# Two attention mixers re-sequenced: score pairs between projections, and latent keys one turn sooner

## The reference, cut to what matters

```python
# differential attention, 8 heads: two score maps per head, one weighted difference
s1 = einsum("bqhd,bkhd->bhqk", q1, k1) * scale
s2 = einsum("bqhd,bkhd->bhqk", q2, k2) * scale
p = softmax(s1) - lam * softmax(s2)
o = einsum("bhqk,bkhe->bqhe", p, v)          # then rms_norm, w_o

# latent attention (MLA), 16 heads, 256 queries, 512 keys
cq, ckv, k_rope = split(h @ w_down, [256, 384])
q = rms_norm(cq) @ w_uq                      # 64 + 32 (rotary) per head
kv = rms_norm(ckv) @ w_ukv                   # 64 key + 64 value columns per head
s = (q_nope @ k_nope + rope(q_rope) @ rope(k_rope)) * scale
o = softmax(s) @ v
```

## Time and profile before

| | us |
|---|---|
| three runs | 2319.05, 2320.97, 2321.87 |
| median | 2320.97 |
| the profiled execution, whole | 2318.96 |
| its span | 2317.1 |
| PE busy | 2124.6 (92%) |
| DVE busy | 1500.3 (65%) |
| ACT busy | 1039.8 (45%) |

### The profile page before, as it was taken

One profiled execution on the slowest core, in us unless ns is written; L12 is line 12 of the kernel. 1 busy time (PEld: TensorE's weight loads), 2 busy tenths in 40 slices (PEclk: granted clock), 3 DMA queues, 4 the chain that ended last, 5 costly groups with the idle time before them and its releaser, 6 DMA issues.

```text
span 2317.1 us, 33662 instructions
## 1 busy us (share of the span) xinstructions
PE 2124.6 (92%) x12966; PEld 1849.5 (80%) x12966; DVE 1500.3 (65%) x2165; ACT 1039.8 (45%) x1740; POOL 7.2 (0%) x30
## 2 busy tenths in 40 slices
PE   5989999998999889999987889997899889999997
PEld 2677888885777768888866679996899787799997
DVE  3358676686666577767777767885766654555554
ACT  4325223235566552322335655554544563444444
POOL 0000000000000000000000000000000000000000
PEclk8999999998999999999988999998999987799998
DMA  9634464442111136458551037671455531355551
GB/s 352 234 116 141 145 206 144 155 136 78 55 55 55 60 141 199 141 189 274 189 134 55 28 119 244 233 238 58 143 185 181 154 109 45 102 173 177 177 179 58
DMA packets 254192, 339.27 MB, mean 146 GB/s; under 512 B 23943, under 2 KB 232162, under 8 KB 254066
## 3 DMA queue, kind: packets, MB, share of 16 engines
q1 hardware_dynamic: 254066, 337.54, 44.2%
HBM read 336.47 MB, written 1.05 MB: 146 GB/s over the span
## 4 chain that ended last, share of the span: by engine, by line
PE 86%; DVE 6%; ACT 5%; issue 2%; DMA 1%; SPq 1%; POOL 0%; DVEq 0%; ACTq 0%
PE bank L1350 26%; PE bank L1351 25%; PE bank L1352 25%; PE bank L1968 4%; DMA mod_raw<-in_mod_w 1%; DVE norm L2048 1%; PE bank L1400 1%; PE bank L1573 1%; PE bank L1412 1%; SPq L530 0%; PE bank L1426 0%; PE bank L1890 0%; PE bank L1891 0%; ACT norm L813 0%; DVE mpt_lo L2506 0%
## 5 line engine op out<-in xcount | busy, mean ns | idle before, releaser
L1350 PE MATMUL bank<-h_hi,w_hi 128*128 128x256 f32 (+3 forms) x2024 | 673.1, 333 | 53.4 <-DVE h_lo L2057 48.6
L781 ACT ACTIVATE w_hi<-w_raw 128x1024 fp32r<-128x1024 f32 x443 | 464.8, 1053 | 525.6 <-PE bank L1352 505.1
L1351 PE MATMUL bank<-h_lo,w_hi 128*128 128x256 f32 (+3 forms) x2024 | 666.4, 329 | 0.0
L1352 PE MATMUL bank<-h_hi,w_lo 128*128 128x256 f32 (+3 forms) x2024 | 665.6, 329 | 0.0
L2024 DVE TENSOR_TENSOR w_lo<-w_raw,w_hi 128x1024 fp32r<-128x1024 f32 x443 | 539.7, 1222 | 172.1 <-ACT w_hi L781 169.6
L1350 PEld LDWEIGHTS bank<-h_hi,w_hi 128*128 128x128 f32 (+1 forms) x2024 | 392.1, 194 | 99.7 <-issue 59.3
L1352 PEld LDWEIGHTS bank<-h_hi,w_lo 128*128 128x128 f32 (+1 forms) x2024 | 391.8, 194 | 32.3
L1351 PEld LDWEIGHTS bank<-h_lo,w_hi 128*128 128x128 f32 (+1 forms) x2024 | 392.4, 194 | 31.0 <-issue 0.2
L1350 PE MATMUL bank<-g_hi,w_hi 128*128 128x512 f32 (+1 forms) x1152 | 391.1, 339 | 4.5 <-DVE g_lo L2341 3.0
L1351 PE MATMUL bank<-g_lo,w_hi 128*128 128x512 f32 (+1 forms) x1152 | 388.4, 337 | 0.0
L1352 PE MATMUL bank<-g_hi,w_lo 128*128 128x512 f32 (+1 forms) x1152 | 388.2, 337 | 0.0
(11 more groups left out here) (356 smaller groups left out, 2363.0 us busy)
## 6 DMA issues: line engine op xcount, KB each, us to landing
w_raw<-in_mlp_w SPq DMA_DIRECT2D x128, 1024.0 KB, 5.7
mod_raw<-in_mod_w SPq DMA_DIRECT2D x128, 768.0 KB, 5.2
w_raw<-in_w_expert_gate SPq DMA_DIRECT2D x16, 1024.0 KB, 5.2
w_raw<-in_w_expert_up SPq DMA_DIRECT2D x16, 1024.0 KB, 5.2
w_raw<-in_w_expert_down SPq DMA_DIRECT2D x16, 1024.0 KB, 4.9
w_raw<-in_diff_w_qkv SPq DMA_DIRECT2D x12, 1024.0 KB, 5.2
w_raw<-in_fourier_w SPq DMA_DIRECT2D x8, 1024.0 KB, 8.3
w_raw<-in_w_in SPq DMA_DIRECT2D x8, 1024.0 KB, 5.8
```

The source lines that it names most:

```text
L781: act.activation(W_hi[n % RING][:, :].rearrange("p (k c) -> p k c", c=P), w_raw[slot][:, :, place, :], ACT.Copy).then_inc(s("w_hi"), 1)
L1350: pe.matmul(dst, w_hi, r_hi, start=start, stop=False)
L1351: pe.matmul(dst, w_hi, r_lo, start=False, stop=False)
L1352: return pe.matmul(dst, w_lo, r_hi, start=False, stop=stop)
```

## The change

Six edits, all in the two mixers.

1. Differential attention, PE: the four score pairs of a head are issued one at a time or two together, as 0, then 1 and 2, then 3, with the panels (and halves of panels, `panel_part`) between them; `turn_weights` now stands in the middle of panel v. `exps` and `mixes` are called for (0,) and (1, 2, 3), and ACT takes the projected q between them.
2. The last head: pairs 0 and 1, `out_products(0)`, pair 2, `out_products(1)`, pair 3, `out_products(2)`; `exps` and `mixes` run over all four in one call.
3. Down projection: the rotary keys are rotated before the reciprocal of the keys' norm, the square sum of the keys is issued in the middle of the third panel, and the queries' reciprocal and table come before the low part of `ckv` and a panel split. ACT's copies move likewise. `query_sum` stands ahead of the first query on PE.
4. The low part of the rotary keys (two 64x512 subtractions) moves from DVE to POOL, between POOL's two rotary swaps of weights.
5. Keys of a pair of heads are projected in the even turn before last instead of the last odd one, and their high and low parts are made half (one head) per turn.
6. `mpt_hi` and `mpt_lo` have two buffers, and on ACT and DVE the copies of the transposed weights come after the output of head t-2.

```diff
-        if turn % 2:
-            add("k", (turn + 1) // 2, "mla_k_lo", turn + 3)
+        if turn % 2 == 0 and turn // 2 + 1 < MLA_HEADS // 2:
+            add("k", turn // 2 + 1, "mla_k_lo", turn + 4)
...
-        mpt_hi, mpt_lo = sb("mpt_hi", [P, 4, LAT], F32R), sb("mpt_lo", [P, 4, LAT], F32R)
+        mpt_hi = [sb("mpt_hi0", [P, 4, LAT], F32R), sb("mpt_hi1", [P, 4, LAT], F32R, over=at["norm0"])]
+        mpt_lo = [sb("mpt_lo0", [P, 4, LAT], F32R), sb("mpt_lo1", [P, 4, LAT], F32R, over=at["norm2"])]
...
             swap_rotary(u, 0)
+            pool.wait_ge(s("kr_hi"), 1)
+            pool.wait_ge(s("uq_swapped"), 1)
+            pool.tensor_tensor(mk_lo[0][HALF:P, :], kr_f[HALF:P, :], mk_hi[0][HALF:P, :].bitcast(F32),
+                               ALU.subtract).then_inc(s("kr_lo"), 1)
...
+            pool.wait_ge(s("kr_lo"), 2)
             swap_rotary(u + 2, 1)
...
                     if on:
-                        exps(h, (0, 1))
+                        exps(h, (0,))
                     take(turn, 0, q_f, HALF ** -0.5)
                     if on:
-                        exps(h, (2, 3))
+                        exps(h, (1, 2, 3))
...
                     if on:
+                        n, t = p0 + 3 * turn, t0 + 3 * turn
                         pe.wait_ge(s("qk_lo"), 2 * h + 2)
-                        scores(h, range(2))
-                        panel_product(p0 + 3 * turn, t0 + 3 * turn, H_hi, H_lo, full)
-                        scores(h, range(2, 4))
-                        panel_product(p0 + 3 * turn + 1, t0 + 3 * turn + 1, H_hi, H_lo, full)
+                        scores(h, [0])
+                        panel_product(n, t, H_hi, H_lo, full)
+                        scores(h, [1, 2])
+                        panel_part(n + 1, t + 1, range(4))
+                        scores(h, [3])
+                        panel_part(n + 1, t + 1, range(4, KT))
+                        panel_part(n + 2, t + 2, range(4))
                         turn_weights(h)
+                        panel_part(n + 2, t + 2, range(4, KT))
...
                     scores(turn)
                     if turn + 1 < MLA_HEADS:
                         query(turn + 1)
+                    if turn % 2 == 0 and turn // 2 + 1 < MLA_HEADS // 2:
+                        keys(turn // 2 + 1)
                     if turn >= 2:
                         weighted_values(turn - 2)
                     if turn:
                         turn_weights(turn - 1)
-                    if turn % 2 and turn + 1 < MLA_HEADS:
-                        keys((turn + 1) // 2)
```

More of the change, by code:

```diff
@@ L1114, in mla_attention @@
                 query(0)
-                keys(0)
+                for j in range(2):
+                    keys(0, j)
                 for turn in range(MLA_HEADS + 2):
@@ L1131, in mla_attention @@
                         query(turn + 1)
[L1132 to L1139, removed]
-                                           ACT.Copy).then_inc(s("pt_hi"), 1)
-                    if turn % 2 and turn + 1 < MLA_HEADS:
-                        keys((turn + 1) // 2)
-                    for i in VALUE_TILES.get(turn, []):
-                        values(i)
+                    if turn // 2 + 1 < MLA_HEADS // 2:
+                        keys(turn // 2 + 1, turn % 2)
                     if on:
@@ L1154, in mla_attention @@
                                        ACT.Copy).then_inc(s("o_hi"), 1)
+                    if 1 <= turn <= MLA_HEADS:
+                        for i in range(2):
+                            done, ps = attention_tile("mla", "turn_p", turn - 1, i)
+                            act.wait_ge(s("aux_done"), done)
+                            if turn >= 3:
+                                act.wait_ge(s("pv_done"), turn - 2)
+                            act.activation(mpt_hi[(turn - 1) % 2][:, 2 * i:2 * i + 2, :].rearrange("p a b -> p (a b)"), ps[:, :],
+                                           ACT.Copy).then_inc(s("pt_hi"), 1)
+                    for i in VALUE_TILES.get(turn, []):
+                        values(i)
                     for n in splits.get(turn, []):
@@ L1649, in diff_attention @@
                 pe.wait_ge(s("qk_lo"), 2 * last + 2)
-                scores(last, range(2))
-                scores(last, range(2, 4))
-                for h in range(O_BATCH - 1):
-                    out_products(h)
+                scores(last, [0, 1])
+                out_products(0)
+                scores(last, [2])
+                out_products(1)
+                scores(last, [3])
+                out_products(2)
                 turn_output(O_BATCH - 1)
@@ L2373, in diff_attention @@
                 last = HEADS - 1
-                mixes(last, (0, 1))
-                mixes(last, (2, 3))
+                mixes(last, range(4))
                 output_lo(O_BATCH - 1)
@@ L2518, in mla_attention @@
                                           G_hi[half, h // 2, 0:LAT].bitcast(F32), ALU.subtract).then_inc(s("o_lo"), 1)
+                    if 1 <= turn <= MLA_HEADS:
+                        for i in range(2):
+                            _, ps = attention_tile("mla", "turn_p", turn - 1, i)
+                            dve.wait_ge(s("pt_hi"), BEFORE_MLA["pt_hi"] + 2 * (turn - 1) + i + 1)
+                            hi = mpt_hi[(turn - 1) % 2][:, 2 * i:2 * i + 2, :].rearrange("p a b -> p (a b)")
+                            lo = mpt_lo[(turn - 1) % 2][:, 2 * i:2 * i + 2, :].rearrange("p a b -> p (a b)")
+                            dve.tensor_tensor(lo, ps[:, :], hi.bitcast(F32), ALU.subtract).then_inc(s("pt_lo"), 1)
+                    for i in VALUE_TILES.get(turn, []):
+                        values(i)
                     for n in splits.get(turn, []):
```

102 lines of the change are left out of this document (50 added, 52 removed).

## The result

The changed kernel takes 2308.76 us (median of 5 runs, 2306.03 to 2309.61), the kernel before on the same chip 2321.77 (5 runs, 2319.05 to 2324.80). The ratio is 0.9942, its 95% interval 0.9928 to 0.9957: 13 us faster, where 18 were forecast. The profiled execution took 2309.61 (span 2307.7, before 2317.1), 9.4 us less than the profiled one of before.

What follows compares the result with a forecast made beforehand. PE, busy 92% of the span, bounds the kernel; gains come from its waits or low clock. Differential 7.2, down projection 3.7 and latent turns 7.0 sum to 17.9 us: 2301.1 profiled, 2303 median, 8-in-10 range 2294 to 2312.

Steps and rivals of the forecast that it cites:

- rival A: Whole kernel: only the plain parts come, clock falls stay, value and split turns give nothing; gain 10.4, 2310.5 us; chance 0.18.
- Differential turns, 4.6 forecast: Differential attention, turns 1 to 7: moving score pairs behind panels removes the 1.67 us v_lo waits; together 4.6 us gained.
- The chain that I walked: Differential turn, ACT and DVE to pt_lo: 0.9 us longer, new PE wait about 1.0 us, plain turn gains 0.45 us.
- turn 5 nothing: Differential turn 5: no gain, since ACT's root and DVE's scaling end last; PE waits 1.06 us for that chain.
- the 2.0 of turn 6: Differential turn 6: credited 2.0 us because PE is late there by the low clock, not by the chain.
- Last head, 2.6: Differential attention's last head: turn_weights about 2.0 us sooner, out_products(3) from 779.81 to 777.15; what follows moves by 2.6 us.
- Down projection, 3.7: Down projection to first latent scores: queries' root starts at 1231.5, root to scores 8.0 us, scores at 1239.5; gain 3.7 us.
- four ones-matmuls take 1.91: Down projection: after queries' squares end at 1229.4, four ones-matmuls take 1.91 us, so the root starts at 1231.5.
- Sixteen turns, 9.1 less 1.5: Latent attention: beat 5.72 us, first to last maximum 107.0 to 97.9, gain 9.1; 1.5 off for returning clock falls.
- B: Latent turns: PE stays at the low clock, turns about 8.5 us; 18 us slower overall, 2339; chance 0.04.
- C: Whole kernel: waits only change places, no effect within 4 us, 2320; chance 0.07.
- D: Whole kernel: PE never falls to the low clock and the differential chain is as PE is; 2294 us; chance 0.09.

Runs made afterwards that it cites:

- e7: Changed kernel plus 16 idle 128x512 matmuls on PE during differential turn 5's wait for the scaled output rows; 2303.28 us, ratio 0.9927.
- e9: Kernel before, order unchanged, with idle matmuls ahead of the latent key waits and five ahead of each second differential score pair; 2308.79 us, ratio 0.9951.
- e1: Kernel before with only the differential attention's new order (edits 1 and 2); 2318.25 us, ratio 0.9985.
- e10: Changed kernel with the two 64x512 rotary key subtractions moved from POOL back to DVE; 2312.15 us, ratio 0.9953.
- e8: Kernel before, order unchanged, with idle 128x512 matmuls ahead of scores that wait for keys in six latent turns; 2318.44 us, ratio 0.9987.
- e6: Kernel before with only the sixteen latent turns' edits (5 and 6); 2318.21 us, ratio 0.9986.
- e11: Changed kernel with turn 5's root and scaling early, idle matmuls ahead of pt_lo waits, turn 5's output transposes and the first latent transposes; 2303.75 us, ratio 0.9917.

## Why the prediction came out as it did

The sign and the range held; the forecast's own range (2297 to 2308) was missed by 0.8 us, and rival A's 2310.5 is nearer to 2308.76 than 2303.

**Differential turns, 4.6 forecast.** The chain that I walked was right: a wait of 0.92 us on `pt_lo` (1.0), scores 26.65 us apart (26.6), turn 7 0.8 shorter (0.95). A plain turn gained 0.36, forecast was 0.45. The step that failed is "turn 5 nothing, since ACT's root and DVE's scaling stand on that chain and end last". The end of that chain indeed didn't move, but PE came three us earlier to it, so the wait of 1.06 became 4.13, and behind it the clock fell: 33.7 us where 30.2 stood. e7 shows how much is the clock (3.6 us in the turn). At the full clock throughout, the new order takes 189.6 us (e7), the old 191.6 (e9): 2 us of real shortening, turn 5 lengthened by 0.8 included. I priced the falls of before as something that goes (the 2.0 of turn 6) and gave the new waits none. The two halves belong together: 2 us of order, and a fall more or less.

**Last head, 2.6.** `turn_weights` against the first scores: 14.6 us where it was 15.75, 1.2 sooner, not 2.0. PE waits 1.11 us there for `p_all`, so the chain of maxima and mixes ends 0.8 later than I walked it; the later score pairs stood behind output products at the low clock (0.80 for a matmul at 767.63), which may be a part of it, and no run tells. Further on 2.0 of the 2.6 us were there (34.00 us into the part instead of 36.04). What took 1.6 of them is the clock behind the `g_lo` wait of 2.16 us: matmuls of 0.63 us, 0.40 before. At the end of the part 0.5 is left. e1's profile has it too (0.80 at that matmul); in e7 and e9 the clock stayed up, and the part took 61.9 and 62.3 us instead of 64.3.

**Down projection, 3.7.** Undersized. The root starts 21.7 us behind the first down panel, 28.4 before: 6.7 sooner, 5.5 forecast. The mis-sized term in it is "four ones-matmuls take 1.91": they took 1.13, and "the clock in this stretch is low in both" was wrong, since from these matmuls to the scores 0.92 were granted. Root to scores takes 7.3 us, not 8.0. Seven profiles with the new order give 29.0 to 30.4 us from down panel to scores, those with the old one 34.3 to 34.7, so 4.8 on average and 5.7 in the profiled execution. The POOL pair took 2.64 us, done at 1230.8, 8.8 us ahead of the scores. The 2.2 us estimated from the Trainium skill (GPSIMD Engine Reference, "Performance versus the Vector engine" and "Specifications") were near; its factor of two too (1.29 us on POOL, 0.69 on DVE for the same 64x512). The sharing that it warns of wasn't put to the test: the page speaks of VectorE instructions with two SBUF inputs or in a 2-port mode, and what ran beside POOL's subtractions was DVE's reciprocal, with one input, and for 0.6 us a multiplication that reads PSUM. The reciprocal takes 3.35 us, and as much in the kernel before and in e10, where POOL subtracts nothing. A panel split on DVE, which does read two SBUF tiles, ran beside POOL's copies behind them (both from 1230.85) and took 1.22 us, as the split at 1235.92 did with nothing on POOL beside it.

**Sixteen turns, 9.1 less 1.5.** 6.2 came in the profile, for another reason than the one I counted most on. The plain beat is 5.87, not 5.72: every other turn has 6.11, in which `mpt_hi` starts 4.27 us behind the first maximum instead of 3.81 (1322.00 and 1327.65). From the third maximum to the last, before took 90.3 us, e1 with the same code and no falls there 84.6, the changed kernel 82.9: 5.7 of the gain is the clock and 1.7 the order, and the first two intervals lose 1.2 (17.8 for 16.7). What the edits take away are waits of 2.36 us behind which the clock fell, and filling those waits with idle matmuls gives the same 3 us of median (e8 and e6). I had named the falls ("a clock at half") as a part; they are the larger part by far. They were also more than the "five of the sixteen turns": eight of the fifteen intervals of before were granted less than 1.00.

**Rivals.** A's condition (the falls stay) is the nearest, though they moved rather than stayed. B needed the low clock throughout: it came in the first two intervals (0.77 and 0.65), and from the third maximum on the changed kernel is granted 1.00. C (waits change places) is true of the turns' waits, if not of the time: 10.2 us for `mk_lo` behind the first scores' 5.9 became 14.1 for `mpt_lo`, 3.4 of it behind the last turn. D needed no fall at all, which none of the kernels shows. The Trainium skill (TensorE: Matmul & The Clock Gate, "HAM oscillation") is right that waits bring the fall, but here most waits of 0.9 to 2.4 us pass without one.

**What stays open.** Why the clock falls behind a 0.9 us wait in four kernels and not in two with the same instructions ahead of it, and why it fell in the latent turns 8 and 10 in three of eight profiles of the new turns. And why the down projection's edits are worth 7.4 us by medians when their stretch is 4.8 us shorter: its profile was its slowest run (2319.16, the others 2311.8 to 2317.1), so the execution that shows it wasn't recorded.

## What to carry to other kernels

Ahead of moving work forward on the engine that bounds, look for the points it must still meet: if what it waits for doesn't move, the gain becomes one longer wait, and a longer wait can cost the clock behind it. Compare stretches of unchanged code between profiles before crediting a gain to an edit; here they differ by 4 to 6 us from the clock alone. And try idle matmuls in the waits first: they separate the wait from the clock, and were worth nearly as much here as the reordering.

## What the runs showed of the hardware

A fall can cost as much as the wait ahead of it: 4.13 us of waiting, then 6.5 us in which 128x128 matmuls took 0.41 instead of 0.28, and a next score pair at 0.79 instead of 0.50. Against e7, where the clock stayed up, that is 3.6 us in the turn and 0.9 in the next. Behind waits that were filled with matmuls of 128x512 whose result is overwritten (16 in 3.8 us), no fall came in e7, e8, e9 or e11; it came behind other waits. The same instruction stream lost its clock at different waits once something far ahead had changed: and even unchanged, turns 1 and 2 took 27.4 and 27.0 us in one profile of before, 25.9 and 28.6 in the other.
